# A two-layer diffusion trunk: last expert pair, layer boundary, order of moved weight chunks and router of layer 0

## The reference, cut to what matters

```python
def rms_norm(x, g):
    xf = x.astype(jnp.float32)
    y = xf * lax.rsqrt(jnp.mean(xf * xf, axis=-1, keepdims=True) + EPS)
    return (y * g.astype(jnp.float32)).astype(x.dtype)

def modulate(x, g, shift, scale):
    return rms_norm(x, g) * (1.0 + scale) + shift
# each layer, for the latent stream (with c) and the context stream (with c_ctx):
#   h = modulate(x, ...);  z = h @ w_in             (four token mixers read slices of z)
#   mixers: differential attention, long convolution with a generated filter,
#           windowed attention, Conformer convolution (31 taps, then a layer norm)
#   acc = sum over branches of sigmoid(z_gate) * (y_branch @ w_branch[b])
#   x = x + gate * (acc @ w_out)
#   h = modulate(x, ...)
#   lg = h @ w_rg;  le = h @ w_re                   (the router: group, then two of its experts)
#   y = sum over the 2 chosen experts of weight * (silu(h @ w1) * (h @ w3)) @ w2
#   x = x + gate * y
```

## Time and profile before

| | before |
|---|---|
| median of 3 runs | 1486.79 us (1486.69 to 1487.41) |
| profiled execution | 1489.83 us |
| its span | 1488.0 us |
| mean granted clock of TensorE | 0.99 |
| TensorE busy | 96% |
| VectorE busy | 54% |
| ScalarE busy | 19% |
| GpSimd busy | 12% |
| transfers | 354.75 MB, 238 GB/s over the span |

### The profile page before, as it was taken

The page is one execution under the profiler, slowest core; times in us unless marked ns, Lnnn a source line. Parts: engine busy times, 40 slices in busy tenths (PEclk is TensorE's granted clock), DMA queues, the critical chain, the costliest instruction groups (busy, mean ns, idle before and its releaser), DMA issues.

```text
span 1488.0 us, 16946 instructions
## 1 busy us (share of the span) xinstructions
PE 1426.5 (96%) x6164; PEld 713.8 (48%) x6164; DVE 797.5 (54%) x1734; ACT 279.0 (19%) x566; POOL 183.3 (12%) x160
## 2 busy tenths in 40 slices
PE   6999999999999999899999998998999999999888
PEld 3444554444444444633333334865787866333332
DVE  3396776787675859534222238789586625121111
ACT  3311111333331300400110113111243202000000
POOL 0000100011212200031111123001011210221110
PEclk9999999999999999999999999999999999999999
DMA  9610124323234344699999995414555686999996
GB/s 379 252 57 28 57 85 149 131 89 113 86 103 145 113 159 155 265 356 419 422 421 423 424 374 218 142 57 175 195 196 198 239 348 248 392 415 415 421 418 253
DMA packets 49664, 354.75 MB, mean 238 GB/s; under 512 B 6288, under 2 KB 6672, under 8 KB 22448
## 3 DMA queue, kind: packets, MB, share of 16 engines
q1 hardware_dynamic: 41792, 330.79, 56.4%
q0 software_dynamic: 4800, 14.24, 2.5%
q10 hardware_dynamic: 2992, 8.65, 1.5%
HBM read 343.88 MB, written 9.78 MB: 238 GB/s over the span
## 4 chain that ended last, share of the span: by engine, by line
PE 81%; DVE 10%; DMA 5%; issue 3%; ACT 1%; SPq 0%; POOL 0%; DVEq 0%; ACTq 0%; POOLq 0%
PE ps L1276 28%; PE ps L1593 20%; PE ps L1460 6%; PE ps L1377 5%; PE ps L1603 5%; PE ps L1289 4%; DMA gates<-w 3%; DVE n_ L2535 2%; PE ps L1614 1%; PE ps L1244 1%; PE ps L1413 1%; DMA ring<-wmod 1%; PE ps L1361 1%; DMA n_<-y_scratch,m 1%; PE ps L1449 1%
## 5 line engine op out<-in xcount | busy, mean ns | idle before, releaser
L1276 PE MATMUL ps<-hT,ring 128*128 128x512 f32 (+1 forms) x1344 | 452.3, 491 | 8.1 <-DVE ssa L2634 3.4
L1276 PEld LDWEIGHTS ps<-hT,ring 128*128 128x128 f32 x1344 | 253.8, 191 | 189.3 <-issue 161.5
L1593 PE MATMUL ps<-ring,m 128*64 128x512 f32 x616 | 276.8, 601 | 5.2 <-DMA n_<-w 3.7
L2446 DVE SCALAR_TENSOR_TENSOR spare<-ring,crow 128x1024 bf16<-128x1024 f32 x128 | 180.0, 1406 | 4.4
L1593 PEld LDWEIGHTS ps<-ring,m 128*64 128x64 f32 x616 | 81.7, 138 | 184.8 <-issue 183.3
L2161 POOL TENSOR_TENSOR wide<-wide,gates 128x512 f32<-128x512 f32 (+1 forms) x48 | 77.9, 1624 | 428.3 <-DVE gates L2627 428.3
L1289 PE MATMUL ps<-ring,hT 128*128 128x512 f32 (+1 forms) x352 | 125.1, 515 | 0.0
L1595 PE MATMUL ps<-n_,m 128*64 128x512 f32 x224 | 103.4, 612 | 0.0
L2204 POOL DMA_INDIRECT m<-h_scratch,m x56 | 53.0, 946 | 347.0 <-DVE m L2295 264.1
L1377 PE MATMUL ps<-yT,ring 128*128 128x512 f32 (+1 forms) x256 | 93.9, 489 | 1.3 <-ACT yT L2001 1.3
L1595 PE MATMUL ps<-wide,m 128*64 128x512 f32 x208 | 93.6, 596 | 0.0
(11 more groups left out here) (423 smaller groups left out, 1705.1 us busy)
## 6 DMA issues: line engine op xcount, KB each, us to landing
ring<-w SPq DMA_DIRECT2D x38, 2048.0 KB, 12.3
ring<-win SPq DMA_DIRECT2D x52, 1024.0 KB, 5.3
ring<-wmod SPq DMA_DIRECT2D x48, 1024.0 KB, 5.2
n_<-w SPq DMA_DIRECT2D x13, 2048.0 KB, 15.5
hT<-w SPq DMA_DIRECT2D x13, 2048.0 KB, 17.3
wide<-w SPq DMA_DIRECT2D x12, 2048.0 KB, 17.0
ring<-wbr SPq DMA_DIRECT2D x8, 1024.0 KB, 4.9
ring<-wout SPq DMA_DIRECT2D x4, 2048.0 KB, 8.1
```

The source lines that it names most:

```text
L1276: last = pe.matmul(b[:, 0:W], w[:, k, jj * P:(jj + 1) * P], hT[:, k, 0:W], start=(k == 0), stop=(k == KD - 1))
L1593: pe.matmul(ps[0:HALF, bnk, :], left[:, k, 0:HALF], even[k], start=(k == 0), stop=(k == n_k - 1), skip_group_check=True)
L2446: last = v.scalar_tensor_tensor(out=spare[:, 0, :].bitcast(BF16), in0=chunk3(cn, 2)[:, block_ % 2, :], scalar=0.5, in1=crow[:, s, :], op0= ...
```

## The change: what it does

**Router of layer 0.** The scales of tiles 0 to 2 and both modulation factors are put ahead of the last `xup`. New steps `hTtwo` and `hTlast` turn tiles by stream: tiles 0 and 1 first (four groups of two column blocks), then tile 2, then tile 3. `lg` and `lgrow` are split into a latent and a context part. `fdft` of parts 0 to 3 is moved from in front of the norm into the places of dummy products behind the row stores, the list and the side list. `at_rank` and `token_of` of layer 0 get other places in the buffer `m`, since `fdftout` fills theirs.

```diff
+def two_engine(k2, s):
+    return ("SVSS", "VSVS")[s][k2]
+def second_norm_steps(l):
+    outs = [[(two_engine(k2, s), ("hTtwoout", l, k2, s)) for k2 in range(KD // 2)] for s in range(2)]
+    normed = norm_steps(l, 2, [TILES - 1])
+    o = [("T", ("hTtwo", l, k2, 0)) for k2 in range(KD // 2)] + normed[:1] + outs[0]
+    o += [("T", ("hTtwo", l, k2, 1)) for k2 in range(KD // 2)] + normed[1:]
+    for k2 in range(KD // 2):
+        o += [("T", ("hTlast", l, k2, 1)), outs[1][k2]]
+    return o + [g for s in range(2) for g in (("T", ("lg", l, s)), ("S", ("lgrow", l, s)))]
...
                 o += [("S", ("sq", l, 2, u)) for u in range(t)] + [("V", ("rstd", l, 2, 0, t))]
+                if with_side(l):
+                    o += [("V", ("scale", l, 2, u)) for u in range(t)] + [("V", ("modfin", l, 2, half)) for half in range(2)]
             o += [("V", ("xup", l, t, hf))]
...
-    o += [g[0] for g in spectrum[1:]]
-    o += [("V", ("scale", l, 2, t)) for t in range(tt - 1)]
-    o += normed[:1] + [g[1] for g in spectrum[1:]] + normed[1:] + modulated_steps(l, 2)
-    o += [("T", ("lg", l)), ("S", ("lgrow", l)), ("T", ("lgT", l)), ("V", ("lgout", l)), ("V", ("picks", l))]
+    if with_side(l):
+        o += second_norm_steps(l)
...
-    o += kept_busy(l, "rank", 2 if with_side(l) else 3)
+    o += spectrum[1] if with_side(l) else kept_busy(l, "rank", 3)
...
-    o += kept_busy(l, "list", 1)
+    o += spectrum[2] if with_side(l) else kept_busy(l, "list", 1)
...
-        o += kept_busy(l, "sidelist", 3)
+        o += [g[0] for g in spectrum[3:]] + kept_busy(l, "sidelist", 1)
```

```diff
                         both_halves(2, xgT, *of_pair("w1", e)).then_inc(gate_done, 1)
+                        if side and not e:
+                            pe.wait_ge(first_side_copied, 1)
+                            turn_side()
+                            spread_rows(5, 0)
```

```diff
+                        sp.wait_ge(last_reader("w2", l), PAIRS - 1)
+                        sp.dma_start(at["w2"][0], pairs_of["w2"][l, PAIRS - 1, 0]).then_inc(at["w2"][1], 16)
                         sp.wait_ge(y_stored, 16 * (PAIRS - 1))
                         sp.wait_ge(side_y_stored, 32 * (PAIRS - 1))
-                        load_pair("w2", PAIRS - 1)
+                        sp.dma_start(odd_at["w2"], pairs_of["w2"][l, PAIRS - 1, 1]).then_inc(odd_landed["w2"], 16)
```

```diff
-    o += [("V", ("scale", l + 1, 1, t)) for t in range(2)] + gated(2) + mixed(3)
-    for pair, gate in zip(turned_pairs(l + 1, 0), [[], [], gated(3)[:1], gated(3)[1:]]):
+    o += [("V", ("scale", l + 1, 1, t)) for t in range(2)]
+    for pair, gate in zip(turned_pairs(l + 1, 0), [[], gated(2)[:1], [], gated(2)[1:]]):
         o += pair + gate
+    o += mixed(3) + [("V", ("early", l, t)) for t in (2, 3)] + gated(3)
     return o + [("V", ("xup2", l, t)) for t in (2, 3)] + [("S", ("sq", l + 1, 1, t)) for t in (2, 3)]
...
-                        for t in (2, 3):
-                            gp.wait_ge(early_summed, t + 1)
-                            nc.gpsimd.tensor_tensor(early_rows[:, t, :], early_rows[:, t, :], gbc[:, 1, :], ALU.mult)\
-                              .then_inc(early_gated, 1)
-                            gp.wait_ge(early_gated, t - 1)
-                            nc.gpsimd.tensor_tensor(x[:, t, :], x[:, t, :], early_rows[:, t, :], ALU.add)\
-                              .then_inc(early_added, 1)
...
+            def early(t):
+                one, two = first_early_rows[:, t, :], early_rows[:, t, :]
+                v.wait_ge(early_scaled, t + 1)
+                v.scalar_tensor_tensor(out=two, in0=two, scalar=early_weight[:, 1, t:t + 1], in1=one,
+                                       op0=ALU.mult, op1=ALU.add).then_inc(early_summed, 1)
+                v.wait_ge(early_summed, t + 1)
+                link(v.tensor_tensor(two, two, gbc[:, t // 2, :], ALU.mult))
+                return v.tensor_tensor(x[:, t, :], x[:, t, :], two, ALU.add)
```

```diff
-        o = pads + context_norm(l)
+        o = context_norm(l) + pads
...
+    o += [g[0] for g in turned([(1, 4)])] if l else []
     o += [s for g in projections for s in g] + [("V", ("rsC", l))] + [s for g in ropes_c for s in g]
-    o += merge(za_groups, turned([(1, 4), (1, 5)] if l else [])) + [("V", ("rsA", l))]
+    if l:
+        o += [s for g in za_groups[:-1] for s in g] + za_groups[-1][:3] + conformer[0][:1]
+        o += [g[0] for g in turned([(1, 5)])] + za_groups[-1][3:] + [("V", ("rsA", l))]
+        conformer[0] = conformer[0][1:]
```

127 lines of the change are left out of this document (70 added, 57 removed).

## The result

The changed kernel takes 1479.42 us (median of 5 runs, 1476.76 to 1481.83) against 1486.81 us for the kernel before: ratio 0.9946, 95% interval 0.9934 to 0.9958. It is 7.4 us faster; 11.6 were forecast. The profiled execution took 1481.83 us with a span of 1480.0, 8.0 less than before. It is the slowest of its five runs, as 1489.83 is above all five of the kernel before. Over 59 later executions of the kernel before, the time went from 1482.56 to 1492.00 us and followed the mean granted clock: 1491.8 us on average at 0.986, 1486.8 at 0.990, 1483.6 at 0.993. A difference of 2 us between medians of few runs is therefore no finding by itself. The stretch from the first turn of the queries to the end, in which TensorE has the same work in all these kernels, shows the size of it: it takes 436.2 to 440.3 us over the 14 traces of this document.

A forecast was written before the change was run, and what follows sets the result against it. TensorE was taken to bound the kernel, improvable only where it stands still or does work off the chain. 5.8 + 0.25 - 1.2 + 6.7 = 11.55 us won gave 1475.2 us; own range 1473.0 to 1477.5, wider range 1471.0 to 1480.5.

The forecast's parts named there:

- the first rival: VectorE sets the pace until attention, so the moved chunks win only the first pause, 3.4 us; 1478.5 us, chance 0.18.
- the slower one: Boundary to first filter tap: VectorE's extra 7.6 us find no cover; 1.5 us slower, 1488.3 us, chance 0.05.
- Router, 5.8 us to the turn: Layer 0's router: transposes start behind the last output product, turn at 604.45 against 610.25; 5.8 us won, bounds 4.6 and 6.4.
- Filter transforms in the place of dummies, 0: Layer 0's router pauses: filter transforms replace dummy products of nearly equal length, so pauses stay as long; 0 us.
- First pair, +0.25: First gate product no longer waits for the side rows' copy; 0.25 us won, bounds -0.2 and +2.0.
- Last pair, 0 for the loads: Last pair: even down matrix issued 7.8 us earlier, odd one arrives earlier, but TensorE does not wait there; 0 us.
- The rival on the stores: Last pair: the even matrix holds pair 6's stores, gathers start up to 2.1 us later; 1477.2 us, chance 0.07.
- The mixing's pause, 0.9, and the transposes 3.5 sooner: Layer boundary: TensorE's 0.91 us pause in the mixing goes, and its transposes begin at 912.95 instead of 916.47.
- Boundary, 1.2 lost: VectorE takes over GpSimd's sums, filter starts at 943.15 against 941.96; 1.2 us lost, bounds 0.5 won and 3.5 lost.
- Moved chunks, 6.7: Layer 1: waits before the first and third gate products go, queries' turn comes sooner; 6.7 us won, bounds 3.4 and 7.2.
- VectorE keeps the pace until attention: Boundary to attention: VectorE's extra 7.6 us leave the moved chunks only 3.4 us; 1478.5 us, chance 0.18.
- Behind it.: From 1064 us to the end: whatever is won before arrives at the end undiminished.

The follow-up runs named there:

- late_w2: The full change, but SyncE issues the first pair's even down matrix only behind the stores of layer 0's token rows; 1480.12 us beside 1487.41, ratio 0.9954.
- no_first: The full change with the first pair as before: side rows turned and spread ahead of the first gate product; 1478.40 us beside 1487.22, ratio 0.9943.
- only_boundary: The kernel before with the boundary part alone, context norm ahead of the clears; 1488.80 us beside 1487.64, ratio 1.0017.
- only_chunks: The kernel before with only the new order of the two moved chunks' steps; 1481.77 us beside 1487.64, ratio 0.9971.
- no_last: The full change with the last pair's loads as before, both down matrices behind the stores; 1481.94 us beside 1487.22, ratio 0.9968.
- busy_boundary: The full change with three dummy products in TensorE's pause ahead of the latent transposes; 1478.27 us beside 1487.41, ratio 0.9946.
- best: Full change minus first-pair part and side-list dummy; first even down matrix later, tile 2's addition earlier, three boundary dummies; 1476.25 us beside 1487.22, ratio 0.9927.

## Why the prediction was right, and where it was not

The time lay inside the stated range, 1471.0 to 1480.5 us, and on the side forecast. But the sum was too large by 4.2 us, and the forecast's own narrower range, 1473.0 to 1477.5, was missed by 1.9. The time is nearest to that of the first rival, 1478.5, whose mechanism did not come: it had the second pause before a gate stay, and both went. So the range held it in part by luck. (Three slips in its working cost less than 0.3 us: 601.60 and 1.02 make 602.6 and not 602.7, 602.7 and 0.98 make 603.7 and not 603.8, and 1475.2 and 2.1 make 1477.3. The cases other than the slower one have a chance of 0.95 together, where "faster" is given 0.91.) By its steps:

- **Router, 5.8 us to the turn.** Measured 5.43, and the transposes stand directly behind the output product. Right. The step that failed is what followed it: I took the list's path as a chain of VectorE and TensorE that moves as a whole, since everything in it hung on the turn. The stores of the token rows are issued 6 us sooner too, but they share the transfer engines with four weight loads whose issue hangs on the output products and did not move. 2.74 us were given back, 1.8 to 2.7 over the seven traces with these loads. The trace of before had the rows for it: the transfer engines' share is 1.00 in the window at 594 to 599 us, and still 0.99 from 606 to 609, where the first store is now issued (606.7). I had asked what the faster chain triggers for SyncE's queue, and not what its own stores collide with.
- **Filter transforms in the place of dummies, 0.** As long as the turn waited for the gather it was hidden. In `late_w2` the turn waits for it: the last two parts and the dummy, at the lower clock, take 5.3 us where the three dummies took 4.2. Over the 12 us that end with this turn the mean granted clock is 0.72 in all eleven kernels with the router part and 0.86 in the three without. No run tells whether the transforms, the shorter router ahead of them or something else lengthens the stretch.
- **First pair, +0.25.** In the full change the length from the main turn to the side gate product falls by 0.3 us, as forecast, but this was measured against the old arrival of the side rows. There they land 1.9 us behind the main rows (630.1 and 628.2), in the new kernel 0.5 (625.4 and 624.9 by the rows above), and their turn would fill TensorE's wait of 0.8 us for the copy of the main rows. So the edit costs 0.85 (`no_first`). The lower clock at the first gate product came again in the profiled run, as I took it; that was luck, since it is absent in eleven of the twelve experiments, `only_boundary` and `only_chunks` with the old order among them.
- **Last pair, 0 for the loads.** 0.66 us (`no_last`): the odd matrix was "nearly late" and the sooner pair loop made it late. The rival on the stores is half true: with the even matrix under way the odd one, which is issued when they have landed, is issued at 876.88 instead of 875.7 with everything else 3.6 us sooner, so they land 4.8 us later than they would, and the gathers are issued 2.4 us later. No cost of it shows, because the odd matrix, alone, is done sooner, and the gathers follow it. This is in accord with the Trainium skill's rule on the order of completion (DMA: Bandwidth & Descriptors, Queues, rings and completion order): stores and even matrix land within 0.2 us of each other. The price that I gave for it was the wrong part.
- **The mixing's pause, 0.9, and the transposes 3.5 sooner.** Both as forecast (12.3 us behind the first mixing product instead of 15.95).
- **Boundary, 1.2 lost.** 1.3 at the same clock (`only_boundary`); 2.2 in the full change's profile, whose stretch at the lower clock was twice as long. Where no stretch came (`no_first`, `busy_boundary`) the filter starts 0.3 us sooner than before; the forecast had 0.5 for that case. I had counted one stretch at this place and bounded the cost at 3.5. The term was right; its condition was luck, since the number of stretches differs from trace to trace.
- **Moved chunks, 6.7.** 5.95. That VectorE's first rotation sets the time of this turn was in the forecast: I had the turn 1.6 us behind the last of three branch products, and it comes 1.8 behind. What failed is the last 0.5 us, taken off for small waits of VectorE that were to go. They did not: the rotation ends 67.7 us behind the turn of the long convolution's input before (1043.29) and 67.9 after (1042.07). The rival "VectorE keeps the pace until attention" is true in that VectorE is the one that the turn waits for, and false in its price.
- **Behind it.** 0.61 us, well inside the 4 us by which this stretch differs from trace to trace. In this pair of profiles what was won before 1064 us reached the end.

Together: 5.43 - 2.74 + 0.38 - 2.19 + 5.95 is 6.8; with 0.56 ahead of the change and 0.61 behind it, 8.0. Of the 4.7 us between 6.8 and 11.55, 2.7 are the gather, 1.0 the boundary's clock, 0.75 the turn of the queries, 0.4 the router.

What stays open: whether the dummy products keep the clock up at the boundary, since the same pause had all three values of it without them; what lengthens the stretch at the lower clock ahead of the first turn; and by how much `best` beats the full change in the median.

## What to carry to other kernels

When a chain on the compute engines is made shorter, list the stores and gathers that it issues itself, and look at the transfer engines' share at their new time: a load whose issue did not move is now in front of them. When an engine takes over work to relieve another, put it where the engine waits: one addition of 3.7 us moved into the wait made 2.1 us won out of 1.3 lost, at the same clock. And an edit that is right for the arrival times of the old kernel has to be costed again with those of the new one; the first pair's order changed its sign by that, the last pair's loads their size.

## What the runs showed of the hardware

- GpSimd's additions beside VectorE's: in the kernel before a 128x1024 sum on VectorE took 2.38 us and the next one 1.81 with GpSimd at work on the same form, and 1.22 without; two factors of 128x8 took 2.40 together and 0.37. By GpSimd's spans, which are rough, its instructions ended at 907.39, 910.69 and 913.99 us and the three slowed steps at 908.48, 911.77 and 914.21, each less than its own length behind. That looks like waiting for a whole instruction of GpSimd rather than like sharing, but no run isolates it. The effect is large; undoing it was still no gain by itself.
- Stores of 512 KB took 3.0 us from issue to landing when the weight loads ahead of them were done, and 5.9 while the loads were still under way, at the same place of nearly the same program.
- A pause of TensorE of 3.3 us was followed by a granted clock of 1.00, 0.93 or 0.86 over the same 24 us in different traces of nearly the same code (`no_first`; `late_w2` and `no_last`; the full change). Over the 59 executions of the kernel before, the mean granted clock of the whole program went from 0.985 to 0.993 with the code unchanged, and between 0.986 and 0.993 the time differs by 8 us.
